# A third seven-product pair in each FFN step, and the additions of the down projection moved from VectorE to accumulating DMAs

## The reference, cut to what matters

```python
x = x + 0.5 * swiglu(rmsnorm(x, ffn1_norm), w_gate1, w_up1, w_down1)
x = x + merged(mixers(rmsnorm(x, mix_norm))) @ w_out
x = x + 0.5 * swiglu(rmsnorm(x, ffn2_norm), w_gate2, w_up2, w_down2)
return rmsnorm(x, final_norm)

def swiglu(x, w_gate, w_up, w_down):
    return (silu(x @ w_gate) * (x @ w_up)) @ w_down
```

## Time and profile before

| quantity | value |
|---|---|
| median of three runs | 2107.01 us |
| the profiled execution's own time | 2106.82 us |
| its span in the trace | 2105.0 us |
| TensorE busy | 99% of the span, mean granted clock 0.997 |
| VectorE busy | 77% |
| ScalarE busy | 52% |
| DMA, mean over the span | 191 GB/s |

### The profile page before, as it was taken

One profiled execution on the slowest core, in us unless ns is written; L12 is line 12 of the kernel. 1 busy time (PEld: TensorE's weight loads), 2 busy tenths in 40 slices (PEclk: granted clock), 3 DMA queues, 4 the chain that ended last, 5 costly groups with the idle time before them and its releaser, 6 DMA issues.

```text
span 2105.0 us, 26528 instructions
## 1 busy us (share of the span) xinstructions
PE 2081.9 (99%) x9475; PEld 1727.4 (82%) x9475; DVE 1611.0 (77%) x1613; ACT 1095.1 (52%) x1259; POOL 2.6 (0%) x7
## 2 busy tenths in 40 slices
PE   8999999999999999999999999999999999999997
PEld 6888888888888888888888888888888888888886
DVE  7988988899888744444455655688998888998886
ACT  6555555554555444554554344465555555555553
POOL 0000000000000000000000000000000000000000
PEclk9999999999999999999999999999999999999999
DMA  7655556555565455545445655556565655465652
GB/s 270 220 189 189 199 199 212 204 177 204 190 209 200 140 182 196 181 160 170 159 154 197 200 198 192 188 185 215 170 212 185 219 203 203 163 219 179 219 204 96
DMA packets 202452, 402.88 MB, mean 191 GB/s; under 512 B 6417, under 2 KB 6593, under 8 KB 202273
## 3 DMA queue, kind: packets, MB, share of 16 engines
q1 hardware_dynamic: 202032, 401.64, 56.2%
q0 software_dynamic: 160, 0.46, 0.1%
q10 hardware_dynamic: 208, 0.08, 0.0%
HBM read 400.06 MB, written 2.10 MB: 191 GB/s over the span
## 4 chain that ended last, share of the span: by engine, by line
PE 95%; DVE 2%; ACT 1%; DMA 1%; issue 1%; SPq 0%; ACTq 0%; DVEq 0%
PE ps L530 21%; PE ps L532 21%; PE ps L531 21%; PE ps L545 6%; PE ps L543 6%; PE ps L544 6%; PE ps L707 3%; PE ps L709 3%; PE ps L708 3%; PE ps L595 1%; DMA raw<-in_ffn_w_gate 1%; DVE w_lo L1201 0%; PE ps L718 0%; PE ps L779 0%; ACT w_hi L922 0%
## 5 line engine op out<-in xcount | busy, mean ns | idle before, releaser
L1201 DVE TENSOR_TENSOR w_lo<-raw,w_hi 128x1024 fp32r<-128x1024 f32 x256 | 312.8, 1224 | 303.4 <-ACT w_hi L922 303.2
L922 ACT ACTIVATE w_hi<-raw 128x1024 fp32r<-128x1024 f32 x256 | 270.2, 1059 | 310.7 <-PE ps L532 310.5
L935 ACT ACTIVATE w_hi<-raw 128x1024 fp32r<-128x1024 f32 x280 | 297.0, 1061 | 221.9 <-PE ps L709 98.7
L1235 DVE TENSOR_TENSOR w_lo<-raw,w_hi 128x1024 fp32r<-128x1024 f32 x280 | 342.1, 1222 | 79.5 <-ACT w_hi L935 66.2
L530 PE MATMUL ps<-w_hi,xT_hi 128*128 128x512 f32 x816 | 321.3, 394 | 2.7 <-DVE w_lo L1201 2.7
L532 PE MATMUL ps<-w_hi,xT_lo 128*128 128x512 f32 x816 | 318.6, 390 | 0.0
L531 PE MATMUL ps<-w_lo,xT_hi 128*128 128x512 f32 x816 | 318.2, 390 | 0.0
L1235 DVE TENSOR_TENSOR more_lo<-raw,more_hi 128x1024 fp32r<-128x1024 f32 x160 | 195.6, 1223 | 43.5 <-ACT more_hi L935 34.1
L935 ACT ACTIVATE more_hi<-raw 128x1024 fp32r<-128x1024 f32 x160 | 169.6, 1061 | 110.7 <-PE ps L532 87.1
L530 PE MATMUL ps<-w_hi,hT_hi 128*128 128x512 f32 x576 | 224.4, 390 | 0.0
L532 PE MATMUL ps<-w_hi,hT_lo 128*128 128x512 f32 x576 | 224.1, 389 | 0.0
(11 more groups left out here) (218 smaller groups left out, 3583.6 us busy)
## 6 DMA issues: line engine op xcount, KB each, us to landing
raw<-in_ffn_w_gate SPq DMA_DIRECT2D x88, 1024.0 KB, 5.0
raw<-in_ffn_w_up SPq DMA_DIRECT2D x88, 1024.0 KB, 5.0
raw<-in_ffn_w_down SPq DMA_DIRECT2D x88, 1024.0 KB, 5.1
raw<-in_w_in SPq DMA_DIRECT2D x80, 1024.0 KB, 5.0
raw<-in_w_out SPq DMA_DIRECT2D x16, 1024.0 KB, 5.0
raw<-in_w_proj_dil SPq DMA_DIRECT2D x8, 1024.0 KB, 5.1
raw<-in_w_proj_fox SPq DMA_DIRECT2D x8, 1024.0 KB, 5.0
xres<-in_x SPq DMA_DIRECT2D x4, 512.0 KB, 7.1
```

The costliest lines, as they stand in the source:

```text
L922: nc.scalar.activation(slot_hi(place, offset), raw_half(place, offset), ACT.Copy).then_inc(hi_ready, 1)
L935: nc.scalar.activation(slot_hi(place, offset), src, ACT.Copy).then_inc(hi_ready, 1)
L1201: nc.vector.tensor_tensor(slot_lo(place, offset), raw_half(place, offset), slot_hi(place, offset).bitcast(F32), ALU.subtract).then_inc(lo_ ...
L1235: nc.vector.tensor_tensor(slot_lo(place, offset), step_source(r)[0], slot_hi(place, offset).bitcast(F32), ALU.subtract).then_inc(lo_ready, 1)
```

## The change

- Three of the four groups (1, 2 and 3) are computed by seven products, group 0 the direct way. A step has 33 slabs: pair stage (0 to 6), pair stage (7 to 13), direct group (14 to 17), pair stage (18 to 24), down (25 to 32). The order of the seven products is T3, gate, T1, T2, up, T4, gate.
- `sums` shrinks to two buffers: T3 and T2 share one, T1 and T4 the other.
- A third set of x sums is made in the first chunk (`sum_pairs`, `round_pairs`, `split_pairs` three times), and the up accumulation is started and ended in other instructions (`direct_up`).
- In all steps but the last of each FFN the additions of the down projection leave VectorE: ScalarE copies the two PSUM banks times 0.5 into one of two halves of `gate_buf`, and GpSimd issues a DMA that adds this buffer (512 KB) to `xres`. The copy into a half waits for the DMA that read it last. The banks are free for TensorE behind the copy.
- The first token half is transposed behind slab 4, the second behind the second pair stage (slab 13). The first of the post-additions (M6 + M1) stands ahead of the split of its slab.
- The hardware loops pass over two steps at a time, since 33 is not a multiple of the ring; 2 x 33 is.

```diff
-FIRST, STEP = 2 * WIDE, 30
+FIRST, STEP = 2 * WIDE, 33
-PAIRED = {0: 0, 11: 1}
-DIRECT = {7: 0, 18: 2}
+PAIR_AT, PAIR_GROUPS, PAIR_SLABS = (0, 7, 18), (1, 2, 3), 7
+DIRECT_AT, DIRECT_GROUP = 14, 0
+DOWN_AT = STEP - DOWN
-PRODUCTS = (("sum", T3), ("up", 1), ("sum", T1), ("sum", T2), ("sum", T4), ("gate", 1), ("gate", 0))
+PRODUCTS = (("sum", T3), ("gate", 0), ("sum", T1), ("sum", T2), ("up", 1), ("sum", T4), ("gate", 1))
+SUM_PLACE = {T3: 0, T2: 0, T1: 1, T4: 1}
-FREE = (-6, -4, -2, 0, 2, 7, 9, 11, 13, 18, 20, 22)
+FREE = (-6, -4, -2, 0, 5, 7, 12, 14, 16, 18, 23, 25)
...
 # TensorE, step
-                    for o in paired(place, 0, 0):
+                    for o in paired(place, 0):
                         if o == 1:
-                            pe.wait_ge(added, base - 1)
-                        if o == 2:
+                            pe.wait_ge(silu_done, i * TT + (silu + TT))
+                        if o == 4:
+                            pe.wait_ge(down_copied, drained - 1)
+                        if o == 5:
                             transpose_tokens(hid, 0, T)
-                        if o == 4:
                             pe.wait_ge(hidden_ready, hid + TT)
-                            pe.wait_ge(added, base)
+                            pe.wait_ge(down_copied, drained)
+                    for o in paired(place, 1):
+                        pass
                     pe.wait_ge(ht_lo, hid + 1)
                     transpose_tokens(hid, 1, T)
...
 # ScalarE, step
+                        if not last and o > DOWN_AT and (o - DOWN_AT) % 2 == 1:
+                            n = (o - DOWN_AT) // 2
+                            earlier = f * (STEPS - 1) + (n >= 2)
+                            act.wait_ge(slab_done, place.slab(o + 1))
+                            if not (type(i) is int and i + earlier == 0):
+                                act.wait_ge(down_added[(n + 2) % NN], i * 16 + earlier * 16)
+                            banks = DOWN_BANKS[n]
+                            nc.scalar.activation(gate_buf[:, n % 2], ps[:, banks:banks + TT], ACT.Copy,
+                                                 scale=0.5).then_inc(down_copied, 1)
...
 # GpSimd
+            for j in range(2 * (STEPS - 1)):
+                for n in range(NN):
+                    pool.wait_ge(down_copied, j * NN + n + 3)
+                    if j > 0:
+                        pool.wait_ge(down_added[n], j * 16)
+                    pool.dma_start(xres[:, :, n * CH:(n + 1) * CH], gate_buf[:, n % 2],
+                                   accum_op=ALU.add).then_inc(down_added[n], 16)
...
 # VectorE: the four weight sums of a pair stage
+            def weight_sum(place, q, pair, which, count):
...
+                if which == T2:
+                    dve.wait_ge(lo_ready, place.slab(base + at + 1))
+                    dve.wait_ge(summed, done + T3 + 1)
+                    made = nc.vector.tensor_tensor(out, sums[:, SUM_PLACE[T3]], gate[:, 0::2, :], ALU.add)
...
+                if kind == "paired" and o in (1, 2, 4):
+                    weight_sum(place, q, pair, {1: T1, 2: T2, 4: T4}[o], count)
+                if r + 1 in PAIR_AT:
+                    weight_sum(place, q, PAIR_AT.index(r + 1), T3, count)
...
 # VectorE, step
-                        if o > STEP - DOWN and o % 2 == 1:
-                            n = (o - (STEP - DOWN)) // 2
+                        if last and o > DOWN_AT and (o - DOWN_AT) % 2 == 1:
+                            n = (o - DOWN_AT) // 2
+                            dve.wait_ge(down_added[n], (f + 1) * (STEPS - 1) * 16)
                             add_down(place, o + 1, n, DOWN_BANKS[n], 0.5)
...
 # VectorE, first chunk
                     if o == 1:
                         sum_pairs(f, 0)
                         scale_x(b, NN - 1)
-                    if o == NN - 1:
-                        split_pairs(f, 0)
-                    if o == WIDE - 3:
-                        sum_pairs(f, 1)
-                    if o == WIDE - 2:
-                        split_pairs(f, 1)
+                    if o in (3, 5, 7):
+                        split_pairs(f, o // 2 - 1)
+                    if o in (4, 6):
+                        sum_pairs(f, o // 2 - 1)
```

More of the change, by code:

```diff
@@ L143, in slot @@
     def slot(self, offset):
+        assert self.per % self.ring == 0
         return (self.start + offset - self.origin) % self.ring
@@ L287, in step_source @@
     def step_source(r):
[L289 to L300, removed]
+        kind, pair, o = step_slab(r)
+        if kind == "paired":
+            what, which = PRODUCTS[o]
+            if what == "sum":
+                return sums[:, SUM_PLACE[which]], None
+            l = PAIR_LOADS[pair][what == "gate"]
+            return raw[:, l % LOADS, which::2, :], l
+        l = DIRECT_LOADS[o // 2] if kind == "direct" else DOWN_LOADS + o // 2
+        return raw[:, l % LOADS, o % 2 * 2:o % 2 * 2 + 2, :], l
     ident = tab[:, C_ID:C_ID + P]
@@ L324, in build @@
     combined = sem("combined")
+    down_copied = sem("down_copied")
+    down_added = [sem(f"down_added{n}") for n in range(NN)]
     hi_ready = sem("hi_ready")
@@ L643, in paired @@
-                    product(place, offset + o, bank, lhs, g == 0, whole and g == 1)
+                    product(place, PAIR_AT[pair] + o, bank, lhs, pair == 0, pair == PAIRS - 1)
             def ffn(f, b):
+                silu = f * FF_CHUNKS * TT
                 def step(place, i, last):
-                    hid, base, merged = i * TT + HID[f], i * NN + ADDED[f], (i + f * STEPS) * COMBINED
-                    for o in paired(place, 0, 0):
+                    hid, merged = i * TT + HID[f], (i + f * STEPS) * COMBINED
+                    drained, base = i * NN + (f * (STEPS - 1) * NN + 2), ADDED[f]
+                    for o in paired(place, 0):
@@ L660, in step @@
+                    for o in paired(place, 1):
+                        pass
                     pe.wait_ge(ht_lo, hid + 1)
                     transpose_tokens(hid, 1, T)
[L662 to L673, removed]
+                    for o in range(2):
+                        slab(place, DIRECT_AT + o, (GATE, GATE + 1), of_x, CT * DIRECT_GROUP + 2 * o,
+                             False, False)
@@ L678, in step @@
                         for o in range(2):
-                            slab(place, STEP - DOWN + 2 * n + o, (banks, banks + 1), of_hidden, 2 * o,
+                            slab(place, DOWN_AT + 2 * n + o, (banks, banks + 1), of_hidden, 2 * o,
                                  o == 0, o == 1)
@@ L691, in ffn @@
                 wide_all(first, WIDE, FIRST_UP)
[L692 to L696, removed]
+                pe.wait_ge(s_lo, (f + 1) * PAIRS)
+                with pe_loop(STEPS // 2 - 1) as i:
+                    for s in range(2):
+                        step(step_place(f, s, 2, i), i * 2 + s, False)
+                step(step_place(f, STEPS - 2), STEPS - 2, False)
+                step(step_place(f, STEPS - 1), STEPS - 1, True)
+                last_down(last_place(f), HID[f] + STEPS * TT, ADDED[f] + NN, 1 if f == 0 else None)
             def direct_up(place, offset, k0, first, last):
@@ L706, in direct_up @@
                         begin = first and j == 0 and t == 1
+                        end = last and j == 1 and t == 1
                         nc.tensor.matmul(acc, hi, hi_w[:, j], start=begin, stop=False)
                         nc.tensor.matmul(acc, hi, lo_w[:, j], start=False, stop=False)
-                        done = nc.tensor.matmul(acc, lo, hi_w[:, j], start=False, stop=last and j == 1)
+                        done = nc.tensor.matmul(acc, lo, hi_w[:, j], start=False, stop=end)
                 done.then_inc(slab_done, 1)
@@ new lines, in step @@
+                        if last and o == DOWN_AT + 4:
+                            for n in (2, 3):
+                                act.wait_ge(down_added[n], (f + 1) * (STEPS - 1) * 16)
+                            round_hidden(i * TT + HID[f] + TT, last_hi, A)
+                for s in range(2):
+                    step(step_place(f, s), s, False)
+                with act.Fori(1, STEPS // 2 - 1) as i:
+                    for s in range(2):
+                        step(step_place(f, s, 2, i), i * 2 + s, False)
@@ L1234, in split_step @@
+                kind, pair, o = step_slab(r)
+                if kind == "paired" and o in (1, 2, 4):
+                    weight_sum(place, q, pair, {1: T1, 2: T2, 4: T4}[o], count)
+                if r + 1 in PAIR_AT:
+                    weight_sum(place, q, PAIR_AT.index(r + 1), T3, count)
+                if r == STEP - 1 and not final:
+                    weight_sum(place, q + 1, 0, T3, count)
                 dve.wait_ge(hi_ready, place.slab(offset + 1))
```

222 lines of the change are left out of this document (113 added, 109 removed).

## The result

The changed kernel takes 2095.88 us (median of four, 2095.43 to 2096.87), the kernel before 2107.02 (2106.81 to 2107.23): ratio 0.9948, 95% interval 0.9936 to 0.9960. It is faster by 11.1 us, where the prediction had 23.6; the time lies in the range, and the likeliest case missed it by 12.5 us. The profiled execution took 2095.74 us, its span 2093.6.

The account below looks back on a forecast made before the run. TensorE's own stream of matmuls was taken as the bound: 2106.8 - 27.2 (fewer matmuls) + 3.4 + 0.2 (first steps of FFN 1 and FFN 2) = 2083.2, against the median 2083.4 us, speedup 1.1%; range 2079 to 2108.

Parts of the forecast that it names:

- Fewer matmuls: One direct group of 48 becomes 42 matmuls: 120 fewer over 20 steps, 27.2 us off TensorE, step 62.1 us.
- VectorE: Per step 58.4 of 62.1 us busy at 1.136 per large instruction, smallest margin 1.0 us; no stall, cost nothing.
- R2: Rival: VectorE becomes the bound, step held at 62.9 us, 2094 to 2097; 12% shared with partly late DMAs.
- The adding DMAs: Down additions by GpSimd: 7 us taken to land, 10.4 allowed before ScalarE's copy is late; sum stays.
- R1: Rival: adding DMA late, ScalarE's copy waits; beyond 10.4 us TensorE loses the excess in 18 steps; slower, 16%.
- ScalarE: Per step about 39 us of 62 busy, copies from PSUM taken at 1.1 us each; costs nothing.
- Weight loads: Issued 6 us or more before the rounding that wants them; TensorE would notice only past 7.5 us; nothing.
- The moved waits: Transposes at slabs 5 and 14, bank and silu waits: multiply done some 7 us before step's end; cost nothing.
- The first step: Third x sums and T3 delay VectorE: TensorE loses 3.4 us in FFN 1 (between 0 and 4.5), 0.2 in FFN 2.
- R3: Rival, no difference: loads, two-step loops or new traffic eat exactly the gain, 1.3 us a step; 4% with R1's edge.

Follow-up runs that it names:

- the first experiment: Changed kernel with the last steps' transposes behind down slab 30 in place of 28, token rounding and splitting one slab later: 2085.23 us, ratio 0.9897.
- the fastest version: Changed kernel with last-step transposes later, first T3 earlier, third x sums behind root and silu, table casts in FFN 1's last step: 2081.36 us, ratio 0.9879.

## Why the prediction was right in the looped steps and wrong in the last

Forecast and result differ by 12.5 us: 10.7 in the last steps, which the sum didn't have at all, and 2.0 in the first steps, sized at 3.6 (3.4 and 0.2) and measured at 5.6 (4.9 less 0.3, and 1.0). The sum of the parts, 27.2 - 10.7 - 5.6 = 10.9, is within 0.2 us of what was measured. That the time still lies in the stated range says nothing for the account of the last steps: the range was made for other losses.

- *Fewer matmuls*: right. 9355 matmuls at the old pace, 1.36 us less per looped step.
- *VectorE*: right. 59.15 us of 62.17, no TensorE wait inside looped steps. R2 fell: at 1.22 per instruction a step couldn't be 62.17 with this load, and the kernel with four more per step ran nearly gapless within 1% of 1.136. The rule of the Trainium skill that spoke against it ("VectorE: DVE Perf Modes", section "The DRAIN you can't avoid") doesn't hold for these instructions; the same section says that a next operation that isn't held starts earlier, and that half, which I hadn't weighed, agrees with the trace (starts 1.13 apart, durations 1.22).
- *The adding DMAs*: right. 5.5 us against 7 taken and a limit of 10.4, which a slower DMA bore out in three steps. The 4.4 us that I had estimated from the Trainium skill's "DMA: Bandwidth & Descriptors" and "Collectives: The Full Stack" is 1.1 too low; the interval of 4.0 to 16.8 from the rows held it at its lower end. R1 fell.
- *ScalarE*: right in effect. The copy took 1.007 us, against 1.1. The total of about 39 us was added up too low: 33 x 1.06 + 4 x 1.1 is 39.4 before the silu, M1 and the token rounds. It measured 40.1.
- *Weight loads*: right in effect. They became 5.2 to 5.4 us from 5.0 to 5.1, under the 7.5 at which TensorE would notice.
- ***The moved waits* ("the multiply is done some 7 us before the step's end ... Nothing"): this step failed.** It is true of the 18 steps whose transposes stand in the next step, and I priced the wait there only, at nothing. In the last step there is no next: both token halves are transposed inside the down slabs, behind slab 28. My own figure would have shown it: four down slabs of 2.72 us, 10.9 us, still follow these transposes, and a multiply done 7 us before the end is 3.9 us late for them; it measured 3.3, twice. The change moved the multiply in VectorE's order from place 23 of 30 to 28 of 33, that is from one slab behind the start of the down slabs to three, and it left the transposes where they were, behind the fourth down slab. At its new place it stands behind an addition and a split that wait for that very slab, so by this order even an emptier VectorE would be late (argued from the queue, not run); the two experiments that move it ahead of one or both took 1.2 and 2.3 us off each wait. Adding by DMA in the last step too, which would take the addition away, was not run. The rows to see it by lay in the trace of before, where the transposes of the last step at 684.83 wait for nothing and the multiply had been started 2.3 us earlier; I had read none from a last step.
- *The clock*: no part of the sum, since I expected no wait long enough to ask. It put some 1.6 us on each of the two waits, and the restart of the matmuls 0.4: 2 x (3.3 + 0.4 + 1.6) = 10.6, against the 10.65 that came back.
- *The first step*: the right place and mechanism, a term too small. Slab 3's split started at 62.34, not 61.6, and the second transposes came 4.9 late, not 3.7. It is not one wait of 3 to 4 us, as forecast, but five of 0.3 to 0.6. FFN 2 lost 1.0 where 0.2 was forecast; the 3.3 us of lateness in that sum has no working beside it. The idea that T3 had lost its gap was right, for FFN 1 at 1.3 us where the sum had 1.1; that it would cost FFN 2 1.0 us was not in the sum.
- *R3* fell: an unchanged kernel time had no mechanism. That the time came out inside R2's span of 2088 to 2103 says nothing for R2, whose waits aren't there.

## What to carry to other kernels

A loop body whose work is consumed an iteration later has an exception: the last iteration, which consumes its own. When an order is rewritten, follow each moved result to its consumer once in the body, once in the first and once in the last iteration; the first and last steps took 16 of 27 us here. Look also at what stands ahead of the moved instruction in its queue: if that waits for the consumer's engine, no spare time helps. And where an engine was filled to 95%, the load showed at the start of the pipeline, and small work put elsewhere returned 1.3 of its 1.5 us.

## What the runs showed of the hardware

- Granted clock of TensorE after a wait inside dense work: after waits of up to 0.6 us (five in the first step) it stayed at 1.00, after 1.05 us too (two of two), after 2.14 and 2.15 us it stayed once and fell to 0.50 once, after 3.3 us it fell all four times (twice in the changed kernel, twice with T3 moved), after 3.5 us both times (additions back on VectorE). The two of the changed kernel read 0.50 from 680.0 to 683.4 and from 2045.3 to 2048.7. The second of the 3.5 us waits reads 0.50 from 2067.3, still inside the wait, to 2074.0, so the slow stretch has no fixed length. A fall cost 1.6 us beside its wait, and the waits of one length with two outcomes show that the length of the wait alone doesn't decide.
- At the start of the kernel the stretch at half pace, near the 2.7 us wait for the first weights, has no fixed length either. Starts are 0.43 apart from 13.81 to 16.80 in the trace of before, and from 13.37 to 17.64 in that of after. So slab 0 of FFN 1's first step started at 59.91 before, at 60.60 after the change and at 59.76 in the first experiment; the last two reached the second transposes at 84.3 and 84.5 all the same, since VectorE set that time. In the fastest version slab 0 is at 60.74 and the second transposes at 81.30, where 60.74 + 5 x 1.36 + 12.73 = 80.3: 0.8 us from the start and 1.0 from what is left of VectorE's lateness are the 1.8 that it lacks to the full 27.2.
- In that stretch of the trace after the change the granted clock reads 1.00 from 13 us on while the starts are 0.43 apart; the trace of before reads 0.50 there at the same pace. The starts are to be believed there.
- A DMA of 512 KB that adds on its way from one SBUF buffer to another landed in 5.5 us (5.3 to 9.2), and kept GpSimd busy for 1.18 us each. With stores of the same size beside it, it took 6.9.
